# A blocked recurrence on one core: the levels of a triangular inverse in two halves, and one group's last product between the next group's first

## What is computed

```python
def step(S, inp):                       # 16 heads of 64, S is 64 x 64 per head
    d_t, k_t, v_t, kk_t, a_t = inp[:5]
    sa = jnp.einsum("bhvk,bhk->bhv", S, -kk_t)
    S = (S * d_t[:, :, None, :] + sa[..., None] * (kk_t * a_t)[:, :, None, :]
         + v_t[..., None] * k_t[:, :, None, :])
    out = jnp.einsum("bhvk,bhk->bhv", S, inp[5]) if emit else None
    return S, out
```

## Time and profile before

| | |
|---|---|
| median of 3 runs | 4003.11 us (3998.9 to 4003.67) |
| span of the profiled execution | 3997.2 us; its time with what lies around the span is not listed |
| PE busy, PEld busy | 3803.5 us (95%), 2814.0 us (70%) |
| DVE, ACT, POOL busy | 2297.2 (57%), 886.4 (22%), 1159.2 (29%) |
| chain that ended last | PE 88%, DVE 5%, ACT 3%, issue 3% |
| the 22 full groups of the recurrent stage | from 2264.09 to 2878.96 us |

### The profile page before, as it was taken

How to read it: one execution, slowest core, us unless ns; L and a number is a source line. 1 busy time by engine, 2 the same in 40 slices (tenths; PEclk the granted TensorE clock), 3 DMA queues, 4 the chain that set the end, 5 groups by cost and what they waited for, 6 DMA issues and landing times.

```text
span 3997.2 us, 77236 instructions
## 1 busy us (share of the span) xinstructions
PE 3803.5 (95%) x33844; PEld 2814.0 (70%) x33844; DVE 2297.2 (57%) x3572; ACT 886.4 (22%) x1689; POOL 1159.2 (29%) x860
## 2 busy tenths in 40 slices
PE   8999999999999999999998888888899999999998
PEld 3588887758888855555555678778757888558445
DVE  4578715657564149936443355555426877662695
ACT  3312100010110020021013444444212222550102
POOL 0144544105445420001441422233013554103202
PEclk9999999999999999999999999999999999999999
DMA  2134223423342212101333311111202333211221
GB/s 81 59 129 151 92 85 127 174 110 137 142 151 87 64 53 63 42 29 64 121 99 127 135 45 44 40 36 36 82 15 77 103 107 104 77 37 56 74 63 53
DMA packets 196056, 336.93 MB, mean 84 GB/s; under 512 B 17040, under 2 KB 149136, under 8 KB 187280
## 3 DMA queue, kind: packets, MB, share of 16 engines
q1 hardware_dynamic: 192000, 321.59, 24.1%
q0 software_dynamic: 3728, 10.49, 1.0%
HBM read 285.91 MB, written 38.80 MB: 81 GB/s over the span
## 4 chain that ended last, share of the span: by engine, by line
PE 88%; DVE 5%; ACT 3%; issue 3%; DMA 1%; SPq 0%; POOL 0%; DVEq 0%; ACTq 0%
PE lin_ps L1025 66%; PE out_ps L1025 8%; PE sum_ps L1025 7%; PE lin_ps L1430 6%; ACT arena L1966 2%; DVE arena L2561 1%; PE sum_ps L1911 1%; DVE rstd L2548 1%; ACT L1966 0%; ACT std L1966 0%; ACT ring L1966 0%; DVE hn L2561 0%; DMA features<-arena 0%; DMA arena<-pos 0%; DVE xs L2556 0%
## 5 line engine op out<-in xcount | busy, mean ns | idle before, releaser
L1025 PE MATMUL lin_ps<-hn,ring 128*128 128x256 f32 (+1 forms) x3520 | 1000.3, 441 | 7.5 <-DVE hn L2561 4.4
L1025 PEld LDWEIGHTS lin_ps<-hn,ring 128*128 128x128 f32 x3520 | 667.2, 190 | 315.7 <-issue 249.2
L1025 PE MATMUL lin_ps<-arena 64*64 64x64 f32 (+5 forms) x10032 | 761.1, 261 | 66.5 <-issue 29.0
L1025 PE MATMUL lin_ps<-arena,ring 128*128 128x256 f32 (+1 forms) x3200 | 769.6, 395 | 11.0 <-DVE arena L3029 9.4
L1025 PEld LDWEIGHTS lin_ps<-arena 64*64 64x64 f32 (+2 forms) x10032 | 578.8, 145 | 180.0 <-issue 93.7
L1025 PEld LDWEIGHTS lin_ps<-arena,ring 128*128 128x128 f32 x3200 | 609.0, 191 | 135.2 <-issue 53.9
L2561 DVE SCALAR_TENSOR_TENSOR arena<-arena,vec 128x512 f32<-128x512 f32 (+2 forms) x491 | 384.5, 858 | 1.1
L1966 ACT ACTIVATE arena<-lin_ps 128x512 f32<-128x512 f32 (+3 forms) x375 | 191.0, 524 | 753.6 <-PE lin_ps L1025 722.3
L3516 POOL TENSOR_TENSOR arena<-ring 128x512 f32<-128x512 f32 x67 | 89.5, 1335 | 896.9 <-PE lin_ps L1025 529.8
L1025 PE MATMUL sum_ps<-arena 64*64 64x64 f32 (+1 forms) x7180 | 315.4, 224 | 32.1 <-issue 23.8
L3516 POOL TENSOR_TENSOR ring<-ring 128x512 f32<-128x512 f32 x67 | 102.9, 1535 | 732.2 <-PE lin_ps L1025 428.9
(11 more groups left out here) (279 smaller groups left out, 4880.1 us busy)
## 6 DMA issues: line engine op xcount, KB each, us to landing
ring<-w_up SPq DMA_DIRECT2D x32, 1024.0 KB, 5.9
ring<-w_down SPq DMA_DIRECT2D x32, 1024.0 KB, 5.2
arena<-w_mod SPq DMA_DIRECT2D x24, 1024.0 KB, 7.9
arena<-w_mod SPq DMA_DIRECT2D x12, 2048.0 KB, 7.6
features<-arena SPq DMA_DIRECT2D x64, 384.0 KB, 6.1
ring<-w_conv_in SPq DMA_DIRECT2D x16, 1024.0 KB, 5.7
ring<-w_attn SPq DMA_DIRECT2D x16, 1024.0 KB, 5.7
ring<-features SPq DMA_DIRECT2D x40, 384.0 KB, 3.4
```

What stands on the lines that cost most here:

```text
L1025: return pe.matmul(out, lhsT, rhs, start=start, stop=stop)
```

## The change

Every z, and every fz with ez, is issued in two halves of four units; z and F copies go by halves too (ACT 128x256, DVE 128x256), each half with semaphore counts of its own. z and fz of a half share a bank, so the two halves lie in two banks. The bonus sums move from fz's bank to that of the outputs (`out_ps`), with a wait for `take_o` ahead, and the next outputs wait for the bonus values. u products stand alone; before, the first feature product stood between their two directions. Two of the four k features of level 2 move into z of level 3. The last ez of a group is interleaved, unit by unit, with z of level 1 of the next group. DVE does m's scaling ahead of E's copy in levels 1 to 4, masks k's second half at the head of level 3, and in level 5 does `take_o`, `mask_b`, the bonus values and the aside before E's copy. ACT takes k's second half in level 3.

```diff
         gram_ps = lin_ps[:, 0, :].rearrange("p (c r) -> p c r", c=2)[:, :, 0:6 * CHUNK]
-        z_ps = lin_ps[:, 1, 0:512].rearrange("p (u t) -> p u t", u=UN)
-        fz_ps = lin_ps[:, 1, 512:1024].rearrange("p (u t) -> p u t", u=UN)
+        z_ps, fz_ps = [[lin_ps[:, 1, 512 * s + 256 * n:512 * s + 256 * n + 256].rearrange("p (u t) -> p u t", u=4) for s in range(2)] for n in range(2)]
         ez_ps = sum_ps[:, 0:512].rearrange("p (u t) -> p u t", u=UN)
         x_ps, u_ps, m_ps = [by_dir(sum_ps[:, 512 + 128 * i:640 + 128 * i]) for i in range(3)]
         o_ps = out_ps[:, 0, :].rearrange("p (u t) -> p u t", u=UN)
         pair_ps = out_ps[:, 1, :]
-        spare_ps = lin_ps[:, 1, 512:1024]
+        spare_ps = out_ps[:, 0, :]
         STORES = 4 * KD
...
                     pe.wait_ge(y_act, 2 * (j - 1))
                 else:
                     pe.wait_ge(v_ev, 2 * j + 2)
+                if j:
+                    pe.wait_ge(o_ev, 3 * j - 1)
                 mm(spare_ps, headones, bon[:, 0:512], True, True).then_inc(b_mm, 1)
                 mm(pair_ps[:, 0:256], headones, bon[:, 512:768], True, True).then_inc(b_mm, 1)
...
                 if l == 1:
                     pe.wait_ge(f_init, G + 1)
-                    pe.wait_ge(gram_act, 6 * G + 3)
+                    pe.wait_ge(gram_act, 6 * G + 1 + 2 * s)
                 else:
-                    pe.wait_ge(f_ready, 4 * G + l - 1)
-                for u in range(UN):
-                    m = crossed(z_ps[:, u, :], nq[G % 2][:, u, :], F_[G % 2][:, u, :])
-                    if also and u in (1, 4):
-                        g = step_o(also - 1, 3, u // 4)
+                    pe.wait_ge(f_ready, f_count(G, l - 1, s))
+
+            def z_unit(G, u):
+                return crossed(z_ps[u // 4][:, u % 4, :], nq[G % 2][:, u, :], F_[G % 2][:, u, :])
+
+            def level_z(G, l, s):
+                await_z(G, l, s)
+                for u in units_of(s):
+                    m = z_unit(G, u)
                 m.then_inc(z_mm, 1)
-                if also:
-                    g.then_inc(o_mm, 1)
-
-            def level_fz_ez(G, l):
-
-                pe.wait_ge(z_ev, 5 * G + l)
-                if l == 1:
+
+            def level_z_feature(G, l, s, key, half):
+
+                await_z(G, l, s)
+                for n, u in enumerate(units_of(s)):
+                    m = z_unit(G, u)
+                    if n == 0:
+                        features(key, G, half, 2 + s, 3 + s)
+                m.then_inc(z_mm, 1)
+
+            def level_z_o(G, l, s):
+
+                await_z(G, l, s)
+                for n, u in enumerate(units_of(s)):
+                    m = z_unit(G, u)
+                    if n % 2 == 0:
+                        g = step_o(G - 1, 3, n // 2)
+                m.then_inc(z_mm, 1)
+                g.then_inc(o_mm, 1)
...
+            def await_ez(G, l, s):
+                pe.wait_ge(z_ev, z_count(G, l, s))
+                if s == 0:
+                    pe.wait_ge(e_ready, 5 * G + l - 1)
+
+            def level_fz_ez(G, l, s):
+
+                if l == 1 and s == 0:
                     pe.wait_ge(e_init, G + 1)
-                    if G and G % 3 == 0:
-                        pe.wait_ge(b_ev, 2 * (G // 3) + 1)
-                pe.wait_ge(e_ready, 5 * G + l - 1)
-                for u in range(UN):
-                    if l < 5:
-                        m = crossed(fz_ps[:, u, :], E_[G % 3][:, u, :], zc[:, u, :])
+                await_ez(G, l, s)
+                for u in units_of(s):
+                    m = crossed(fz_ps[u // 4][:, u % 4, :], E_[G % 3][:, u, :], zc[:, u, :])
                     e = heads(ez_ps[:, u, :], zc[:, u, :], E_[G % 3][:, u, :])
-                if l < 5:
-                    m.then_inc(fz_mm, 1)
-                e.then_inc(ez_mm, 1)
+                m.then_inc(fz_mm, 1)
+                if s:
+                    e.then_inc(ez_mm, 1)
+
...
+            def last_ez_first_z(G, s):
+
+                await_ez(G, 5, s)
+                await_z(G + 1, 1, s)
+                for u in units_of(s):
+                    e = heads(ez_ps[:, u, :], zc[:, u, :], E_[G % 3][:, u, :])
+                    m = z_unit(G + 1, u)
+                if s:
+                    e.then_inc(ez_mm, 1)
+                m.then_inc(z_mm, 1)
...
+                    if G == 0:
+                        pe.wait_ge(b_ev, 1)
+                    elif (G + 1) % 3 == 0 and G + 1 < GROUPS:
+                        pe.wait_ge(b_ev, 2 * ((G + 1) // 3) + 1)
...
             for half in range(2):
                 ready_b(0, half)
                 features(0, 0, half)
+            for s_ in range(2):
+                level_z(0, 1, s_)
             for G in range(GROUPS):
                 last = G + 1 == GROUPS
                 for l in range(1, 5):
-                    level_z(G, l)
+                    for s_ in range(2):
+                        if l == 3:
+                            level_z_feature(G, l, s_, 1, 1)
+                        elif l > 1:
+                            level_z(G, l, s_)
                     if G:
                         chain_xo(G - 1, l - 1)
-                    level_fz_ez(G, l)
-                    if l < 3:
-                        ready_k(G, l - 1)
-                        if G:
-                            chain_u_features(G - 1, l - 1, 1, G, l - 1)
-                        else:
-                            features(1, G, l - 1)
-                    elif last:
+                    for s_ in range(2):
+                        level_fz_ez(G, l, s_)
+                    if G:
                         chain_u(G - 1, l - 1)
-                    elif l == 3:
+                    if l == 1:
+                        ready_k(G, 0)
+                        features(1, G, 0)
+                    elif l == 2:
+                        ready_k(G, 1)
+                        features(1, G, 1, 0, 2)
+                    elif l == 3 and not last:
                         ready_ends(G + 1)
-                        if G:
-                            chain_u_ends(G - 1, 2, G + 1)
-                        else:
-                            ends(G + 1)
-                    else:
+                        ends(G + 1)
+                    elif l == 4 and not last:
                         ready_b(G + 1, 0)
-                        if G:
-                            chain_u_features(G - 1, 3, 0, G + 1, 0)
-                        else:
-                            features(0, G + 1, 0)
+                        features(0, G + 1, 0)
                     if G:
                         chain_m(G - 1, l - 1)
                     aside(G, l)
                 if G:
                     await_o(G - 1, 3)
-                level_z(G, 5, also=G)
+                    level_z_o(G, 5, 0)
+                else:
+                    level_z(G, 5, 0)
+                level_z(G, 5, 1)
                 if not last:
                     ready_b(G + 1, 1)
                     features(0, G + 1, 1)
                 aside(G, 5)
-                level_fz_ez(G, 5)
+                for s_ in range(2):
+                    if last:
+                        last_ez(G, s_)
+                    else:
+                        last_ez_first_z(G, s_)
             G = GROUPS - 1
             for c in range(4):
...
-
-                act.wait_ge(z_mm, 5 * G + l)
-                copy(zc, z_ps).then_inc(z_ev, 1)
+            def take_z(G, l, s):
+
+                act.wait_ge(z_mm, z_count(G, l, s))
+                copy(zc[:, 4 * s:4 * s + 4, :], z_ps[s]).then_inc(z_ev, 1)
             def chain_x(G, c):
...
             key_squares(1)
             for G in range(GROUPS):
                 for l in range(1, 6):
-                    take_z(G, l)
+                    for s_ in range(2):
+                        take_z(G, l, s_)
                     if G and l < 5:
                         chain_x(G - 1, l - 1)
+                    if l == 3:
+                        take_k(G, 1)
+                    if G and l < 5:
                         chain_u(G - 1, l - 1)
-                    if l < 3:
-                        take_k(G, l - 1)
+                    if l == 1:
+                        take_k(G, 0)
                     if l == 4 and G % 3 == 1 and G // 3:
                         out_root(G // 3 - 1)
...
                 mask_b(0, half)
             for G in range(GROUPS):
                 last = G + 1 == GROUPS
-                for l in range(1, 6):
-                    if l < 5:
-                        level_f(G, l)
-                    if G and l == 5:
-                        take_o(G - 1)
+                for l in range(1, 5):
+                    if l == 3:
+                        mask_k(G, 1)
+                    for s_ in range(2):
+                        level_f(G, l, s_)
+                    if G:
+                        chain_m(G - 1, l - 1)
                     level_e(G, l)
-                    if G and l < 5:
-                        chain_m(G - 1, l - 1)
```

(52 more changed lines are left out.)

27 lines of the change are left out of this document (18 added, 9 removed).

## The result

The changed kernel takes 4011.88 us (median of 8 runs, 4004.15 to 4021.28), the kernel before in runs beside it 3994.42 (8 runs): **ratio 1.0036, interval 1.0024 to 1.0048, 14 us slower**. In a second set of runs the same kernel came to 1.0046 (1.0032 to 1.006). The medians lie 17 us apart; the text goes by the ratio and its interval. The forecast was 4002.0, one microsecond less than before: the time lies within the range, but the sign is wrong.

What follows compares the result with a forecast made beforehand. Group ends and the levels one and two behind them were taken as bound by PE's work and waits, third and fourth levels by instruction supply. 4003.1 + 4.2 (starts) − 3.8 (features, u) − 1.5 (halves) = 4002.0 us, range 3983 to 4017.

Steps and rivals of the forecast that it cites:

- First of three groups: First fz/ez pair after a first group's end waits for DVE's E copy until 2515.99, before 2515.50: 0.5 us later.
- The two other starts: First fz/ez pairs after the second and third of three groups: 0.1 us later and 0.05 earlier.
- 0.1 later: Start behind the second of three groups: E copy done at 2541.0, where the pair started at 2540.90 before.
- 0.05 earlier: Start behind the third of three groups: E copied by 2570.25, where the pair started at 2570.30 before.
- DVE's queue is the new bound: Rival: level five's E copy behind an aside in every group, 0.5 late at 23 starts, +11.5 us, 4014.6; chance 0.20.
- The merged product: At group ends, e and z interleaved cost PE 1.16 us and not 1.84: 0.68 off its work per group.
- DVE is in time: Rival: E is copied right behind the merged product, 0.6 us per group, −14 us, 3984 with other terms; chance 0.17.
- Features and u: Two level 2 features moved to level 3, −1.1 us per three groups; exposed u products, +0.6; together −3.8 us.
- Halves: z halves let the pair start after half of a late ACT copy, −1.5 us; F halves cost nothing.
- Instruction supply: Third and fourth levels are bound by instruction fetch, about 3.59 us per block of 256; saved PE time worth nothing there.
- fetch is not a bound: Rival: blocks come as fast as used, PE's own work counts in every level, −19 us, 3984; chance 0.11.

Runs made afterwards that it cites:

- run 1: Changed kernel with E's copy of level 5 put ahead of the aside in DVE's list: 3987.95 us, 0.9988 of the kernel before.
- run 2: Changed kernel without the mean's small 128x12 multiplication, its factor applied in the centring instruction, order left: 3986.72 us, 0.9987 of the kernel before.
- best: Changed kernel with E's copy ahead of the aside, the mean's factor folded, ACT's second decay exponential behind the copy of x: 3984.20 us, 0.9981.
- run 7: Changed kernel with E's copy ahead, plus four unused products per group: in level 3 3992.15 us, 1.0012; in level 1 instead 4002.67 us, 1.0037.
- e_copy_ahead: The kernel of run 1: changed kernel with E's level 5 copy ahead of the aside, 3987.95 us, 0.9988 of the kernel before.
- run 3: Kernel before with only E's copy of level 5 moved behind mask and aside in DVE's list: 4002.74 us, 1.0035.

## Why the prediction was wrong

**The step that failed** is "First of three groups", with its sum 2513.45 + 0.41 + 0.97 + 0.43 + 0.73. The mechanism was right: E's copy is last in DVE's queue, and the pair starts when it ends. The term 0.43 was wrong. It was read from one row as the price of a 128x12 instruction, and was what had been left of POOL's instruction when DVE came to it; started earlier, it took 1.63. The mark was there to be read: 0.43 is as much as the line's neighbours take for 128x256, and the same line takes 0.17 at two other places of the same trace. From the end of the fourth level's fz to the end of the first pair's fz, PE's records give 9.93 before, 12.06 and 11.62 in two profiles of the changed kernel (mean of seven groups each): 1.7 to 2.1 more, not 0.5. The 1.2 by which the small instruction exceeds its 0.43 turn the 0.5 into 1.7; the rest, up to 0.4, may be the slower pair.

With 1.63 at six starts the forecast's −1 becomes about +6; measured are +14, with an interval of 10 to 19. So the mis-sized term gives the sign and about half of the size. That the rest hangs on the same place, runs 1 and 2 show, since either edit takes back 19 us; how it splits stays open.

**The two other starts** were sized well: "0.1 later" and "0.05 earlier" came out 0.1 to 0.2 earlier (9.21 before, 9.10 and 8.98) and 0.1 earlier (10.26; 10.11 and 10.20). The rival "DVE's queue is the new bound" named the mechanism and nearly the price, 11.5 us for the 14 measured, but with 0.5 at all 23 starts in place of some 2 at a few: that the sums come close is luck. That its time, 4014.6, lies near 4011.88 says less still, as it starts from the higher median. Its weight of 0.20 was too low; I had priced every step of that queue from one row each.

**The merged product**: 1.16, as forecast, and worth nothing, as the sum had it ("What counts is when the next group's first fz/ez pair starts"). "DVE is in time" fell: even with DVE's order mended (run 1) and ACT's too (best), undoing the merge costs nothing.

**Features and u**: −3.8 forecast, −6 measured. **Halves**: −1.5 forecast, −6 measured. Both terms are right in sign; with intervals of 5 us it is not shown that they were too small. **Instruction supply**: run 7 supports it for level 3 by halves; "fetch is not a bound" does not fit, since then both places would cost the same. That a block takes 3.59 us "however dense its matmuls are" was not in the rows: the three windows of the earlier trace rows have the same density, PE busy 2.75 to 2.84, and the window just ahead of them, with as many instructions and PE busy 3.50, takes 4.08:

```profile
2379.82:2383.90 4.08, 3.50 (x128) 3.21 (x129) 1.44 (x5) 1.06 (x4) 0.00 (x0) 1.00 0.30 100
```

The parts do not add up exactly: e_copy_ahead gains 0.12%, while its features and halves are worth 0.16% and 0.14%. So 0.18% is lost somewhere else in the change, or is the sum of three intervals; that stays open.

## What to carry to other kernels

The duration of a short instruction in a profile is not its price until it has been compared with its other occurrences and with what the engine next to it was doing: here the same instruction took 0.17 us with POOL idle, 0.43 and 1.63 with POOL busy, and then always ended with POOL's. When a product is made earlier or shorter, put the copy that its successor waits for ahead of everything on that engine that nobody waits for; here one line of order was worth 19 us, and the whole restructuring with the order mended 5 to 8. And a lower clock behind a wait was here a sign of the wait: filling the wait with work held the clock and brought no time back.

## What was not expected of the hardware

A DVE TENSOR_SCALAR on 128x12 numbers in SBUF is held until a running POOL instruction ends, and counts as busy, not as waiting: it ended 0.03 to 0.04 us behind POOL's instruction at six of six places in the profiles of the kernel before and of the changed one, while the TENSOR_REDUCE ahead of it kept its 0.94. After 2.97 us without a product, the granted clock of TensorE fell from 1.00 to 0.50 at these starts, and was back 3 to 6 us after the pair had started. In the two profiles of the changed kernel it fell behind ten of eleven such waits, in the changed kernel without the merged product (2.38 to 2.40 us) behind four of five, in run 3 (2.20 to 2.25 us) behind two of six. Holding the clock up with a filler left the time as it was (1.0046 and 1.0046), with some 3 us that the filler may have cost itself.
